# Second mixer: the inverse key norms spread as high and low fp32r parts, in pairs between value columns

## The chip, the cores and the metric

The kernel runs on one core of one Trainium2 chip. The metric is the device time of one execution in microseconds (us); lower is better. Five engines work side by side and meet at semaphores: TensorE (PE; its weight loads are listed apart as PEld), VectorE (DVE), ScalarE (ACT), GpSimd (POOL) and SyncE (SP), which issues the DMAs here.

## The reference, cut to what matters

The kernel computes a two-layer encoder trunk on 256 tokens of width 1024. Layer 0 mixes with a long convolution and windowed attention, layer 1 with a bidirectional RWKV-7 scan; each mixer stands between two half-step feed-forward blocks. The change lies in the mixer of layer 1, in how the keys `kk` are normalised by head (16 heads of 64 channels):

```
kk = (k * k_k).reshape(B, L, H, N)
kk = kk / maximum(norm(kk, axis=-1, keepdims=True), 1e-12)
...
k_dir = k * (1 + (a - 1) * k_a)      # a: two directions
b_dir = kk * a
```

`-kk` and `b_dir` enter the scan that follows, `v` too.

## The kernel before

**Precision.** Most products are computed from fp32 numbers that are split into two fp32r parts: a high part (a rounding copy) and a low part (the number less its high part). `three` (L246 to L248) issues the three matmuls high·high, high·low and low·high. Weights come through `raw` by DMA, one step of three blocks of 1024 columns at a time; ScalarE or VectorE writes the high part `WH` (L189, L195; L2159, L2160), VectorE or GpSimd the low part `WL` (L201, L2168, L210). A matmul of plain fp32 operands appears in the trace as two passes.

**The second mixer's projections** (`pe_mix1`, `act_mix1`, `dve_mix1`) run in the order of blocks written out by hand in `MIX1_ORDER` (L38): keys k0 to k7, receptances r0 to r7, the first halves l0 to l3 of the low-rank nets, values v0 to v7 and the second halves x0, x1 (`pe_lora_out`), with v3 and v4 woven into these. A step is three blocks, so x0 lies in step 7, x1 in step 8, and v5, v6, v7 are the last, ninth step. Each value block k adds, for all eight column groups m of 128, three matmuls into the banks `VB`; `pe_row_block` calls a hook `wait(m // 2)` before every second group.

**The norms.** TensorE sums the squares of a head after r6 (L1450); VectorE limits them (L2253), ScalarE takes the root (L2107), VectorE the reciprocal into `RN[:, 1, :]` (L2237): 16 rows, one for each head, of 256 tokens. `pe_spread_norms` (L1411 to L1416) spreads them: for each of eight tiles j of 128 channels, a 16×128 selector `selt` of ones and zeros times the 16×256 reciprocals gives a 128×256 tile in the banks `XB`. It does all eight in a row, in plain fp32, before the last two column groups of v5 (hook n == 3). `removal_keys` on VectorE (L2267) scales the keys with them, two tiles a call, after waiting until `kk_bc` counts those tiles.

**What stands around it.** ScalarE goes through steps n = 2 to 9: at n = 8 the two low-rank hiddens (`hidden`, L2066 to L2070), the split of a weight step (L189, L195), two high parts of inputs (L2050), the sigmoid of the gate's hidden rows (L2110), then 16 sigmoids of x0 (`decays`, L2080); behind the loop 16 more of x1, the high part of the weights of step S_O, and the operands of the scan's tile 0. TensorE's x0 waits before its fifth product until all four hidden pieces are there (`hid_ready`, 4), and before every later group of four for the sigmoids of the group that used its bank.

VectorE's queue behind the loop is: the prefix sums of tile 0, the gate's low parts (L2481, L2485, after ScalarE's high part of step S_O), `removal_keys` for tiles 0 to 3, then the operands of scan tile 0: b (L1838), k (L1841), alpha (L1861), query (L1869), `removal_keys` for tiles 6, 7, 4, 5 (L2267) and the bonus product (L1845). GpSimd scales b and k behind VectorE (L2007, L2012, L2014) and then makes a low part of weights (L210). TensorE's first scan tile (L1481) needs alpha, query, scaled b and ScalarE's first copy of V out of the banks (L2128, after v7). VectorE masks its two products (L1916), and the scan goes on from there, tile after tile, with VectorE and TensorE in turn.

The memory of `HX[:, 4:8]` lies unused by the inputs in this mixer; the squares of the keys and then the operands of tile 0 (among them the prefix sums, alpha, query and b) have their places in it.

Of the kernel before, what the change touches and what calls it, by code (L numbers as in the profile page):

```python
# [15 lines left out]
P = 128  # L16
C = 1024
L = 256
CT = C // P
# [78 lines left out]
def build(nc, io):  # L98
    fp32 = mybir.dt.float32
    f32r = mybir.dt.float32r  # L100
    ALU = mybir.AluOpType
# [4 lines left out]
    with ctx:  # L106
        def sb(name, shape, dt=fp32):
            return ctx.enter_context(nc.sbuf_tensor(name, shape, dt))

        def sem(name):  # L110
            return ctx.enter_context(nc.semaphore(name))
# [3 lines left out]
        HX = sb("HX", [P, CT, 2, L], f32r)  # L115
# [32 lines left out]
        def ccols(name, n, off=0):  # L148
            return cst[:, CC[name] + off:CC[name] + off + n]
# [491 lines left out]
        RN = sg[0:16, :, :]  # L641
# [5 lines left out]
        selt = ccols("selt", CT * P)[0:16, :].rearrange("p (j c) -> p j c", c=P)  # L647
# [650 lines left out]
        def by_unit(a):  # L1298
# [4 lines left out]
        xt_ready, xt_hh, xt_hl = sem("xt_ready"), sem("xt_hh"), sem("xt_hl")  # L1303
        k_read, rp_read, va_read = sem("k_read"), sem("rp_read"), sem("va_read")
        omk_ready = sem("omk_ready")
        hid_ready = sem("hid_ready")
        lr_done = sem("lr_done")
        lr_ready = sem("lr_ready")
        lr_hi, lr_lo = sem("lr_hi"), sem("lr_lo")
        kk_sq, kk_ss, kk_max, kk_root, kk_rec, kk_bc, kk_ready = (sem(f"kk_{n}") for n in  # L1310
                                                                "sq ss max root rec bc ready".split())
# [20 lines left out]

        LEAD = 4
        WINDOW = {2: (6, 7, 8), 3: (9, 10), 4: (11, 12), 5: (13, 14), 6: (15, 16), 7: (17, 18), 8: (19, 20), 9: (21, 22, 23)}
        KB, RB4, VB = bank[4:8], bank[0:4], [bank[6], bank[7], bank[0], bank[1]]
        LB, XB = bank[4:6], bank[2:6]

        def pair_half(bs, j):
            return bs[j // 2][:, (j % 2) * L:(j % 2) * L + L]
# [9 lines left out]
        def pe_row_block(pe, slot, b, outs, i, k, wait=None):  # L1349

            for _ in pe_row_steps(pe, slot, b, outs, i, k, wait):
                pass
# [43 lines left out]
        def pe_square_sums(pe):  # L1396

            for k in range(CT):
                if k % 2 == 0:
                    pe.wait_ge(pair_sq, k // 2 + 1)  # L1400
                last = nc.tensor.matmul(stats_bank(4)[:, 0:L], ones, XSQ[:, k, :], start=k == 0, stop=k == CT - 1)
            last.then_inc(st_ready, 1)
# [5 lines left out]
            wait_block(pe, s, b)  # L1408
            yield from pe_row_steps(pe, s % 2, b, VB, 2 * CT + k, k)

        def pe_spread_norms(pe):  # L1411

            pe.wait_ge(kk_rec, 1)
            pe.wait_ge(lr_ready, 32)
            for j in range(CT):
                nc.tensor.matmul(pair_half(XB, j), selt[:, j, :], RN[:, 1, :], start=True, stop=True).then_inc(kk_bc, 1)  # L1416

        def pe_mix1(pe):
            pe_square_sums(pe)
            for g, (name, k) in enumerate(MIX1_ORDER):  # L1420
                s, b, k = S_RKV + g // 3, g % 3, int(k)
                slot = s % 2
                if name == "v" and k in (3, 4):
                    continue
                wait_block(pe, s, b)
                if name == "k":
                    pe_row_block(pe, slot, b, KB, k, k)
                elif name == "r":
                    pe_row_block(pe, slot, b, RB4, CT + k, k)
                elif name == "v":  # L1430
                    wait = None
                    if k == 0:

                        pe.wait_ge(kk_max, 1)
                        wait = lambda n: pe.wait_ge(rp_read, n - 1) if n >= 2 else None
                    if k == 5:
                        wait = lambda n: pe_spread_norms(pe) if n == 3 else None
                    pe_row_block(pe, slot, b, VB, 2 * CT + k, k, wait)
                elif name == "l":
                    if k == 0:  # L1440
                        pe.wait_ge(k_read, 2)
                    pe_lora_in(pe, slot, b, k)
                else:
                    pe_lora_out(pe, slot, b, k, pe_value_steps(pe, 3 + k))
                if (name, k) == ("r", 6):

                    pe.wait_ge(k_read, 4)
                    pe.wait_ge(kk_sq, CT)
                    for j in range(CT):
                        last = nc.tensor.matmul(KB[2][0:16, 0:L], sel[:, j, :], KSQ[:, j, :], start=j == 0, stop=j == CT - 1)  # L1450
                    last.then_inc(kk_ss, 1)
            pe.wait_ge(kk_ready, 2)
            pe.wait_ge(va_read, 1)
            tiles(lambda t, p, c, a: pe_tile(pe, t, p, c, a))


            for i in range(NCH):
                pe_r_whole(pe, CT - 1, 1, i)
                pe_o(pe, i // 2, (4 * (i % 2), 4 * (i % 2) + 1))
                pe_u(pe, CT - 1, i)  # L1460
                pe_o(pe, i // 2, (4 * (i % 2) + 2, 4 * (i % 2) + 3))
                pe_s(pe, CT - 1, 1, i)
                pe_y(pe, CT - 1, 1, i)
                if i < 3:
                    pe_spread(pe, i + 2)
            pe_groupnorm(pe)
# [364 lines left out]
        def dve_kb_wait(dve, t):  # L1831

            dve.wait_ge(ka_ready, t + 1)
            if not (isinstance(t, int) and t < 2):
                dve.wait_ge(tr_done, 3 * t - 3)

        def dve_b(t, p, z):
            return nc.vector.tensor_tensor(BB[p][:, z * L:(z + 1) * L], tile_of(AG, t, z), tile_of(KK, t), ALU.mult)  # L1838
# [198 lines left out]
        def act_mix1(act):  # L2037
            A, cp = nc.scalar.activation, ACT.Copy
# [46 lines left out]
            for n in range(2, RKV_STEPS):  # L2085
                if n == 4:
                    act.wait_ge(blocks_done, past(SLOT[CT - 1]))
                    for j in range(4):
                        A(K[:, 2 * j * L:(2 * j + 2) * L], KB[j][:, :], cp).then_inc(k_read, 1)
                if n == 8:  # L2090
                    hidden()
                if n < 9:
                    next_hi(act, S_RKV + n)
                if n == 7:
                    act.wait_ge(blocks_done, past(SLOT[2 * CT - 1]))
                    for j in range(4):
                        A(R[:, 2 * j * L:(2 * j + 2) * L], RB4[j][:, :], cp).then_inc(rp_read, 1)
                for i in WINDOW[n]:
                    hi(i)
                if 3 <= n < 7:  # L2100
                    for j in (2 * n - 6, 2 * n - 5):
                        hi_triple(j)
                if n in (4, 5):
                    squares(range(4 * n - 16, 4 * n - 12))
                if n == 6:
                    act.wait_ge(kk_max, 1)
                    A(RN[:, 0, :], KSQ[0:16, 0, :], ACT.Sqrt).then_inc(kk_root, 1)  # L2107
                if n == 8:
                    for m in range(2):
                        A(GS[:, m, :], pair_half(LB, 2 + m), ACT.Sigmoid).then_inc(hid_ready, 1)  # L2110
                    decays(0)
                    act.wait_ge(hid_ready, 4)
                    A(GH[:, :, :], GS[:, :, :], cp).then_inc(lr_hi, 1)
# [28 lines left out]
        def dve_mix1(dve, own):  # L2142
            V_ = nc.vector
            tt, ts, stt = V_.tensor_tensor, V_.tensor_scalar, V_.scalar_tensor_tensor
# [87 lines left out]
            for n in range(2, RKV_STEPS):  # L2232
                for i in WINDOW[n]:
                    mix(i)
                if n == 7:
                    dve.wait_ge(kk_root, 1)
                    V_.reciprocal(RN[:, 1, :], RN[:, 0, :]).then_inc(kk_rec, 1)  # L2237
                if n == 8:
                    for i in range(2):
                        dve.wait_ge(lr_hi, i + 1)  # L2240
                        tt(PL[:, i, :], HID[:, i, :], PH[:, i, :].bitcast(fp32), ALU.subtract).then_inc(lr_lo, 1)
                low(n)
                for i in WINDOW[n]:
                    lo(i)
                if 3 <= n < 7:
                    for j in (2 * n - 6, 2 * n - 5):
                        lo_triple(j)
                if n < 6:
                    for j in (2 * n - 4, 2 * n - 3):
                        mix_triple(j)  # L2250
                if n == 6:
                    dve.wait_ge(kk_ss, 1)
                    ts(KSQ[0:16, 0, :], KB[2][0:16, 0:L], 1e-24, None, ALU.max).then_inc(kk_max, 1)  # L2253
# [20 lines left out]
            dve.wait_ge(lr_ready, 32)  # L2274
            dve.wait_ge(rp_read, 4)
            dve_kb_wait(dve, 0)
            own(dve_b(0, 0, 0))
            dve_b(0, 0, 1).then_inc(bb_ready, 1)
            own(dve_k(0, 0, 0))
# [502 lines left out]
```

## Time and profile before

| | |
|---|---|
| median of 3 runs | 1232.78 us (1232.63 to 1235.1) |
| the profiled execution: its time | 1232.91 us |
| its span, first to last instruction | 1231.1 us |
| busy: TensorE, VectorE, ScalarE, GpSimd | 97%, 65%, 53%, 33% of the span |
| mean granted TensorE clock | 0.993 |

Times in the rows are us from the span's start. A matmul's duration in a row is longer than the distance to the next start, because matmuls overlap; the distance between starts is what a stream costs. In a row of the timeline, "x8" is eight instructions in a row merged into one, and a bracket at the end tells how long the engine stood idle before them and what ended that. The granted clock of 1.00 is 2.4 GHz and 0.50 is 1.2 GHz.

### The profile page before, as it was taken

The numbers are of one execution on the slowest core, as the hardware profiler recorded it, in microseconds if no ns is written. First come the engines' busy times: TensorE is split into PE (matmuls) and PEld (weight loads), VectorE is DVE, ScalarE is ACT, GpSimd is POOL, SyncE is SP. The second block draws the span as 40 slices with busy tenths as digits, with TensorE's granted clock in tenths as the row PEclk, the third lists the DMA queues.
The fourth block names the chain that finished last, engine by engine and source line by source line (L and its number), as shares of the span: only waits on it lengthen the run. The fifth ranks groups of instructions, "written<-read, shape, count | busy, mean of one in ns | idle before, by whom it ended". The sixth has DMA issues, their size and how long they took to land.

```text
span 1231.1 us, 27446 instructions
## 1 busy us (share of the span) xinstructions
PE 1195.8 (97%) x11182; PEld 1084.4 (88%) x11182; DVE 797.2 (65%) x1265; ACT 655.2 (53%) x1114; POOL 403.2 (33%) x218
## 2 busy tenths in 40 slices
PE   8999999988999999999999989998999999999998
PEld 6899999876989999999999979987999889999998
DVE  7655555788585555485555569878777758755554
ACT  5545444654275454474545446684666654554452
POOL 0343443311123434424343410005343412334433
PEclk9999999999999999999999989999999999999999
DMA  9345455422255454555545434411000025554452
GB/s 364 142 167 204 166 191 205 154 103 104 103 205 180 178 204 163 195 208 203 187 170 204 165 142 156 184 73 54 4 4 3 3 75 189 206 201 174 184 200 90
DMA packets 18657, 188.04 MB, mean 153 GB/s; under 512 B 2064, under 2 KB 2576, under 8 KB 3600
## 3 DMA queue, kind: packets, MB, share of 16 engines
q1 hardware_dynamic: 18576, 186.87, 41.2%
q8 instruction: 61, 1.00, 0.3%
q14 instruction: 20, 0.16, 0.0%
HBM read 185.82 MB, written 1.05 MB: 152 GB/s over the span
## 4 chain that ended last, share of the span: by engine, by line
PE 84%; DVE 9%; ACT 5%; issue 1%; DMA 0%; SPq 0%; DVEq 0%; ACTq 0%
PE gu_bank L267 24%; PE gu_bank L269 12%; PE bank L246 7%; PE bank L248 7%; PE bank L247 7%; PE bank L1481 7%; PE gu_bank L246 4%; PE gu_bank L247 3%; PE gu_bank L248 3%; PE gu_bank L1481 3%; DVE WL L201 2%; PE gu_bank L1512 2%; ACT WH L189 2%; DVE HX L407 1%; PE bank L940 1%
## 5 line engine op out<-in xcount | busy, mean ns | idle before, releaser
L210 POOL TENSOR_TENSOR WL<-raw,WH 128x1024 fp32r<-128x1024 f32 x96 | 325.7, 3393 | 587.0 <-ACT WH L195 565.4
L267 PE MATMUL gu_bank<-HX,WH 128*128 128x512 f32 x1280 | 455.6, 398 | 1.2 <-DVE PL L548 1.2
L269 PE MATMUL gu_bank<-HX,WL 128*128 128x256 f32 x1280 | 359.5, 281 | 0.0
L201 DVE TENSOR_TENSOR WL<-raw,WH 128x2048 fp32r<-128x2048 f32 (+1 forms) x113 | 242.9, 2149 | 123.3 <-ACT WH L189 123.3
L267 PEld LDWEIGHTS gu_bank<-HX,WH 128*128 128x128 f32 x1280 | 240.7, 188 | 57.5 <-DVE PL L548 1.8
L269 PEld LDWEIGHTS gu_bank<-HX,WL 128*128 128x128 f32 x1280 | 241.9, 189 | 0.0
L189 ACT ACTIVATE WH<-raw 128x2048 fp32r<-128x2048 f32 (+1 forms) x113 | 203.0, 1797 | 23.4 <-PE gu_bank L248 14.4
L246 PE MATMUL bank<-PH,WH 128*128 128x256 f32 (+1 forms) x720 | 202.3, 285 | 0.0
L247 PE MATMUL bank<-PL,WH 128*128 128x256 f32 (+1 forms) x720 | 201.6, 283 | 0.0
L248 PE MATMUL bank<-PH,WL 128*128 128x256 f32 (+1 forms) x720 | 201.5, 283 | 0.0
L246 PE MATMUL gu_bank<-HX,WH 128*128 128x256 f32 x464 | 137.4, 296 | 3.2 <-DVE HX L407 3.0
L246 PEld LDWEIGHTS bank<-PH,WH 128*128 128x128 f32 (+1 forms) x720 | 135.2, 190 | 4.9 <-ACT work L2110 0.2
L467 ACT ACTIVATE work<-gu_bank 128x512 f32<-128x512 f32 x80 | 48.0, 600 | 170.1 <-PE gu_bank L269 170.1
L248 PEld LDWEIGHTS bank<-PH,WL 128*128 128x128 f32 (+1 forms) x720 | 135.4, 190 | 0.0
L247 PEld LDWEIGHTS bank<-PL,WH 128*128 128x128 f32 (+1 forms) x720 | 135.4, 190 | 0.0
L533 DVE TENSOR_TENSOR gu_bank<-gu_bank,work 128x512 f32<-128x512 f32 x80 | 56.0, 700 | 119.7 <-ACT work L467 119.1
L247 PE MATMUL gu_bank<-HX,WH 128*128 128x256 f32 x464 | 132.0, 284 | 0.0
L248 PE MATMUL gu_bank<-HX,WL 128*128 128x256 f32 x464 | 131.7, 284 | 0.0
L195 ACT ACTIVATE WH<-raw 128x1024 fp32r<-128x1024 f32 x113 | 118.3, 1047 | 0.0
L472 ACT ACTIVATE work<-gu_bank 128x256 f32<-128x256 f32 x84 | 32.3, 385 | 128.6 <-DVE gu_bank L543 128.6
L246 PEld LDWEIGHTS gu_bank<-HX,WH 128*128 128x128 f32 x464 | 89.6, 193 | 9.8 <-issue 5.6
L247 PEld LDWEIGHTS gu_bank<-HX,WH 128*128 128x128 f32 x464 | 89.8, 193 | 0.4 <-issue 0.2
(314 smaller groups left out, 1808.9 us busy)
## 6 DMA issues: line engine op xcount, KB each, us to landing
raw<-stream_in SPq DMA_DIRECT2D x114, 1536.0 KB, 6.4
cst<-const_in SPq DMA_DIRECT2D x1, 1600.0 KB, 17.3
X<-xT_in SPq DMA_DIRECT2D x1, 1024.0 KB, 5.9
raw<-stream_in SPq DMA_DIRECT2D x1, 1024.0 KB, 7.9
arena<-hconst_in SPq DMA_DIRECT2D x2, 512.0 KB, 11.2
out<-X SPq DMA_DIRECT2D x4, 256.0 KB, 2.1
arena<-hconst_in SPq DMA_DIRECT2D x1, 768.0 KB, 14.2
arena<-fw_in SPq DMA_DIRECT2D x1, 512.0 KB, 8.7
```

The costliest lines, as they stand in the source:

```text
L189: nc.scalar.activation(WH[:, slot, :cut], raw[:, slot, :cut], ACT.Copy).then_inc(hi_ready, 1)
L195: nc.scalar.activation(WH[:, slot, cut:end], raw[:, slot, cut:end], ACT.Copy).then_inc(hi_last, 1)
L201: nc.vector.tensor_tensor(WL[:, slot, :cut], raw[:, slot, :cut], WH[:, slot, :cut].bitcast(fp32), ALU.subtract).then_inc(lo_ready, 1)
L210: (eng or nc.gpsimd).tensor_tensor(WL[:, slot, cut:end], raw[:, slot, cut:end], WH[:, slot, cut:end].bitcast(fp32), ALU.subtract).then_inc ...
L246: nc.tensor.matmul(out_ap, wh, xh, start=start, stop=False, **kw)
L247: nc.tensor.matmul(out_ap, wh, xl, start=False, stop=False, **kw)
L248: return nc.tensor.matmul(out_ap, wl, xh, start=False, stop=stop, **kw)
L267: nc.tensor.matmul(out[:, :], WH[:, slot, w:w + P], HX[:, x, :, :].rearrange("p i t -> p (i t)"), start=k == 0, stop=False)
L269: return nc.tensor.matmul(out[:, L:2 * L], WL[:, slot, w:w + P], HH[:, x, :], start=False, stop=k == CT - 1)
L467: nc.scalar.activation(gus[o], gu_bank[:, o, :, L:2 * L], ACT.Copy).then_inc(gx_ready, 1)
L533: nc.vector.tensor_tensor(gated, gu_bank[:, o, :, 0:L], gus[o], ALU.add).then_inc(gsum_ready, 1)
L1481: last = nc.tensor.matmul(dst[r, cols], w[r], x[r], start=start, stop=stop)
```

## The change

The reciprocals are split into a high part `RNH` (a rounding copy on ScalarE) and a low part `RNL` (a subtraction on VectorE); the selector is copied to fp32r as `SELR` on ScalarE. All three lie in the first 16 partitions of `HX[:, 4:8]`. A spread is then two fp32r matmuls into one sum, and the eight spreads are issued in pairs: before the last two column groups of v5, and before the first, third and fifth column group of v6. Since `SELR` and the parts lie where VectorE later writes b, alpha and query, VectorE waits for all eight spreads (`kk_bc`, 8) before it writes b.

```
+        spent = HX[0:16, 4:8, :, :].rearrange("p k i t -> p (k i) t")
+        RNH, RNL, SELR = spent[:, 2, :], spent[:, 3, :], spent[:, 4:8, :].rearrange("p j (i c) -> p (j i) c", c=P)
...
-        def pe_spread_norms(pe):
-            pe.wait_ge(kk_rec, 1)
-            pe.wait_ge(lr_ready, 32)
-            for j in range(CT):
-                nc.tensor.matmul(pair_half(XB, j), selt[:, j, :], RN[:, 1, :], start=True, stop=True).then_inc(kk_bc, 1)
+        def pe_spread_norms(pe, js):
+            if js[0] == 0:
+                pe.wait_ge(kk_parts, 3)
+                pe.wait_ge(lr_ready, 32)
+            for j in js:
+                nc.tensor.matmul(pair_half(XB, j), SELR[:, j, :], RNH, start=True, stop=False, skip_group_check=True)
+                nc.tensor.matmul(pair_half(XB, j), SELR[:, j, :], RNL, start=False, stop=True, skip_group_check=True).then_inc(kk_bc, 1)
...
                     if k == 5:
-                        wait = lambda n: pe_spread_norms(pe) if n == 3 else None
+                        wait = lambda n: pe_spread_norms(pe, (0, 1)) if n == 3 else None
+                    if k == 6:
+                        wait = lambda n: pe_spread_norms(pe, (2 * n + 2, 2 * n + 3)) if n < 3 else None
...
                 if n == 8:
+                    act.wait_ge(kk_rec, 1)
+                    A(RNH, RN[:, 1, :], cp).then_inc(kk_parts, 1)
+                    A(SELR, selt, cp).then_inc(kk_parts, 1)
                     for m in range(2):
                         A(GS[:, m, :], pair_half(LB, 2 + m), ACT.Sigmoid).then_inc(hid_ready, 1)
                     decays(0)
...
+                if n == 9:
+                    dve.wait_ge(kk_parts, 2)
+                    tt(RNL, RN[:, 1, :], RNH.bitcast(fp32), ALU.subtract).then_inc(kk_parts, 1)
...
             dve_kb_wait(dve, 0)
+            dve.wait_ge(kk_bc, CT)
             own(dve_b(0, 0, 0))
```

## Rows read from the trace of the kernel before

**Rows 1.** Chain of waits, 780 to 880 us: start, us, engine, output, line

```profile
824.41 1.92 PE gu_bank L1416 x8
...
838.55 1.98 PE gu_bank L1481 x32
```

**Rows 2.** Windows: stretch, us, busy us and count by engine, granted clock, DMA

```profile
824.28:828.70 4.42, 4.42 (x18) 3.50 (x16) 3.73 (x7) 4.39 (x7) 0.00 (x0) 0.77 0.00 0
828.70:833.70 5.00, 5.00 (x23) 4.51 (x22) 4.97 (x11) 1.31 (x4) 3.74 (x3) 0.52 0.00 0
833.70:837.82 4.12, 4.12 (x35) 3.92 (x33) 3.49 (x5) 0.00 (x0) 3.25 (x2) 1.00 0.00 0
...
246.00:248.00 2.00, 2.00 (x10) 1.67 (x10) 2.00 (x2) 0.00 (x0) 0.00 (x0) 1.00 0.00 0
...
298.00:299.00 1.00, 0.00 (x0) 0.00 (x0) 0.53 (x3) 0.64 (x4) 0.00 (x0) 1.00 0.00 0
```

**Rows 3.** Timeline of TensorE around the spreads: start, duration, line, output<-inputs, shape, count

```profile
824.13 0.28 PE L248 MATMUL gu_bank<-HX,WL 128*128 128x256 f32 x1
...
829.19 0.58 PE L246 MATMUL gu_bank<-HX,WH 128*128 128x256 f32 x1
...
837.54 0.28 PE L248 MATMUL gu_bank<-HX,WL 128*128 128x256 f32 x1
```

**Rows 4.** Timeline of TensorE in x0, where 64-row and 128-row weights take turns

```profile
805.93 0.39 PE L246 MATMUL bank<-PH,WH 64*128 64x256 f32 x2
...
806.28 0.28 PE L248 MATMUL bank<-PH,WL 64*128 64x256 f32 x2
806.49 0.39 PE L246 MATMUL bank<-HX,WH 128*128 128x256 f32 x1
806.71 0.28 PE L247 MATMUL bank<-HX,WH 128*128 128x256 f32 x1
806.83 0.28 PE L248 MATMUL bank<-HX,WL 128*128 128x256 f32 x1
```

**Rows 5.** Timeline of ScalarE in step 8, and its first copy of V

```profile
802.24 1.06 ACT L195 ACTIVATE WH<-raw 128x1024 fp32r<-128x1024 f32 x1
803.19 0.72 ACT L2050 ACTIVATE HX<-work 128x256 fp32r<-128x256 f32 x2
803.93 1.28 ACT L2110 ACT_TABLE_LOAD   x1
805.22 0.66 ACT L2110 ACTIVATE work<-bank 128x256 f32<-128x256 f32 x2
...
837.86 0.60 ACT L2128 ACTIVATE arena<-gu_bank 128x512 f32<-128x512 f32 x1 [6.53 <-PE gu_bank L248]
```

**Rows 6.** Timeline of VectorE from step 9 to the first masks of scan tile 0

```profile
812.60 1.23 DVE L2159 CAST WH<-raw 128x2048 fp32r<-128x2048 f32 x1 [4.92 <-PE bank L248]
...
824.84 1.23 DVE L2481 TENSOR_TENSOR WL<-raw,WH 128x1024 fp32r<-128x1024 f32 x1 [2.64 <-ACT WH L189]
...
827.47 1.66 DVE L2267 SCALAR_TENSOR_TENSOR arena<-arena,par,gu_bank 128x256 f32<-128x256 f32 x4
829.04 0.76 DVE L1838 TENSOR_TENSOR scan<-arena 128x256 f32<-128x256 f32 x2
...
831.17 2.26 DVE L1869 TENSOR_TENSOR scan<-arena,XSQ 128x256 f32<-128x256 f32 x2
...
835.03 2.19 DVE L1845 SCALAR_TENSOR_TENSOR XSQ<-arena,par,XSQ 128x256 f32<-128x256 f32 x1
839.68 0.42 DVE L1916 TENSOR_TENSOR scan<-gu_bank,cst 128x256 f32<-128x256 f32 x1 [2.45 <-PE gu_bank L1481]
840.55 0.42 DVE L1916 TENSOR_TENSOR scan<-gu_bank,cst 128x256 f32<-128x256 f32 x1 [0.45 <-PE gu_bank L1481]
```

**Rows 7.** Timeline of GpSimd: its split behind the operands of tile 0

```profile
834.54 2.40 POOL L210 TENSOR_TENSOR WL<-raw,WH 128x1024 fp32r<-128x1024 f32 x1
```

**Rows 8.** All instructions of line L1845: duration in ns, least, median, most

```profile
L1845 DVE SCALAR_TENSOR_TENSOR XSQ<-arena,par,XSQ x8: 475/480/2195, 835.0 to 976.4; 128x256 f32<-128x256 f32 x8
```

More of the change, by code:

```diff
@@ L1305, in build @@
         omk_ready = sem("omk_ready")
+        kk_parts = sem("kk_parts")
         hid_ready = sem("hid_ready")
```

## The prediction

> **What bounds the kernel now.** I began with the chain of waits over the second mixer's projections. Up to 838 us it is nearly all TensorE, and the eight spreads of the inverse norms stand in it [rows 1]: eight fp32 passes of 256 columns take 1.92 us, 0.24 each, where an fp32r matmul of that width starts every 0.12 us [rows 4]. The windows view shows a second cost: the granted clock falls from 1.00 to a mean of 0.77 in the stretch of the spreads and 0.52 in the next 5.00 us, while TensorE is never idle, and is back at 1.00 after 833.70 [rows 2]; 0.50 is the lower of the two levels, 1.2 GHz. In TensorE's timeline the last column before the spreads starts at 824.13 and the first behind them at 829.19, 4.94 us later than the pitch of 0.12 would put it; the other 53 starts of v5 to v7 take 8.35 us where 53 × 0.12 is 6.36, so the low clock costs 2.0 us more [rows 3].
>
> Then the stretch's other engines. From 838.55 the chain is the first scan tile on TensorE, then VectorE [rows 1]. VectorE's timeline shows its slack: it finishes its operands of tile 0 at 837.22 (835.03 + 2.19), waits 2.45 us for the tile's first product, and 0.45 us for the second [rows 6]. **Those 2.9 us are all that an earlier TensorE can give here**; then VectorE is the bound, unless it gets earlier too.
>
> **The change part by part.** *Sixteen fp32r matmuls for eight fp32 ones*, in four bursts of four. Their own pitch is bounded by 0.12 and 0.24 us; I take 0.12, since the 64-row fp32r pairs stream at it too. But a burst changes the height of the weights from 128 rows to 16 and back. At the nearest such change, 64 to 128 rows, starts stand 0.21 and 0.22 us apart before 0.12 returns [rows 4], 0.19 us lost per change; bounds 0 and 0.19, and I take 0.19, as the fp32 passes came no sooner than 0.21 us after a 128-row matmul either (0.28 in the chain's modelled ends, 824.13 to 824.41) [rows 1, 3]. Counted from 824.13: the last of the sixteen is the 34th start, behind seven changes: 34 × 0.12 + 7 × 0.19 = 5.41, so 829.54, ended at 829.82. The 36 remaining value matmuls and the eighth change bring the last start to 834.05 and V's end to 834.33, against 837.82 (837.54 + 0.28) [rows 3]: 3.49 us earlier, with the clock at 1.00 throughout.
>
> *Two copies on ScalarE*, ahead of the gate's sigmoid in step 8. By the split of 1024 columns (802.24 to the next start at 803.19) the selector's copy is 0.95 us; by two copies of 256 in 0.72, the norms' is 0.36 [rows 5]. Sixteen partitions save nothing I can see; together 1.3 us, bounds 0.7 and 1.5. Nothing hides it: ScalarE runs copies, a table load to 805.21 and the sigmoids to 805.88 without a gap [rows 5], and TensorE's fifth low-rank product starts at 805.93, because it waits for all hidden rows [rows 4]. So TensorE's low-rank blocks, both rounds of sigmoids queued on ScalarE, the split of the next weights behind them and VectorE's work behind that all come 1.3 us later: VectorE waits 2.64 us for that split before 824.84 [rows 6]. The wait for the reciprocal ahead of the copies costs nothing; VectorE made it a step earlier.
>
> *One subtraction on VectorE* (16×256) in step 9: the 4.92 us that VectorE idles before its cast at 812.60 hide it [rows 6]; without that cover about 0.4 us.
>
> *TensorE's wait for the parts* replaces that for the reciprocal and is long met. *The pair-wise order* lets the first keys' scaling begin as before, at 827.47: VectorE is busy with the gate's low parts until then [rows 6], so it never waited for the spreads.
>
> *VectorE's new wait for all eight spreads* stands before the b operands, which start at 829.04 [rows 6]. With the last spread ended at 829.82 they wait 0.78 us (0 without change losses). Queued behind are the k, alpha and query operands, the remaining keys and the bonus product; GpSimd's operands wait for the b operands, and TensorE's tile for alpha and query (833.43 = 831.17 + 2.26, + 1.3 + 0.78 = 835.51).
>
> **Sum.** VectorE is ready for tile 0 at 837.22 + 1.3 + 0.78 = 839.30. TensorE: V ends at 834.33 + 1.3 = 835.63; from V's end to the tile now takes 0.73 us (837.82 to 838.55, through ScalarE's first copy of V [rows 1, 5]), so 836.36, its first product 1.13 us later (838.55 to 839.68) at 837.49, the second 0.87 after it. VectorE therefore comes last. Its first mask moves from 839.68 to 839.30, 0.38 us, and the second's wait of 0.45 goes: **0.83 us gained**. From there the chain is VectorE's and only shifts. The profiled execution took 1232.91 us (span 1231.1 and 1.8 around it), 0.13 above the median of 1232.78; 1232.08 by its own clock, 1232.0 as a median. What can be told from no change here is about 0.2%, 2.5 us.
>
> **What decides beyond that.** The clock's fall came with TensorE busy for all 4.42 us of the stretch [rows 2]. The Trainium skill, "TensorE: Matmul & The Clock Gate", section "HAM oscillation — how this bites in real kernels", ties such falls to gaps in which TensorE idles; the trace disagrees with it here. By that rule the spreads are not the cause, and the low clock would stay: the second rival's time.
>
> VectorE's bonus product takes 2.195 us here against a median of 0.480 [rows 8], and ends just after GpSimd's split (834.54 + 2.40 = 836.94) [rows 6, 7]. It is held by GpSimd; both follow from the b operands and move together, so I keep it. The Trainium skill, "SBUF — State Buffer", section "Who interferes with whom", states a lock that goes to whoever issues first; the trace agrees.
>
> **Rivals.** *The hold dissolves*: if VectorE reaches the bonus product before 834.54's split, that is 0.5 us earlier relative to GpSimd, 1.72 us go: 2.55 gained, 1230.2. Against it: nothing in the change moves them apart. *TensorE decides*: V's lead lands whole, 2.2 us with the copies on the path, 3.5 with them hidden: 1229.3 to 1230.6. For it: the spreads stand in the chain; against it: VectorE's 837.22, which the change only delays.
>
> *The last pair comes late, slower than before.* Place: VectorE's new wait. If 16-row fp32r passes cost 0.24, the change does not do what it says, and four bursts come 4 × 4 × 0.12 = 1.92 us later: 1.09 lost, 1233.9. If instead the clock falls among them as now (0.77 over 4.42 us is 2.0 us at 0.50, so from about 826.7), what is left to 829.54 doubles: 2.9 later, 2.0 lost, 1234.8. It decides once the last spread is more than 0.83 us later than summed. For it: the fall under 16-row passes; against: ten such passes around 246 us left the clock at 1.00 [rows 2], and the bursts are 0.5 us each.
>
> *The stall lowers the clock*: TensorE now idles 1.3 us at the sigmoids; 6.8 us at half speed (2.0 + 0.48 × 2 × 5.00) cost 3.4, and all engines follow: 2.6 lost, 1235.4. Against it: a whole idle us at 298 left 1.00 [rows 2].
>
> **Chances.** The sum 0.62 (own range 1230.6 with both losses at their low ends, 1232.4 with the copies at 1.5 and a median as noisy as now); TensorE decides 0.10; the hold dissolves 0.08; late last pair 0.15; stall 0.05. A range of 1229.9 to 1235.0 leaves out half of TensorE's case and the stall, with margins some 0.13. Faster by over 0.2% means below 1230.3: half of each fast rival and a margin, 0.13. Slower, above 1235.25: the stall and a tail of the late pair, 0.08. The rest, 0.79, is no change.
>
> **Right or wrong.** Right if the granted clock stays at 1.00 from 824 to 838; V ends some 2.2 us earlier; ScalarE's sigmoid starts 1.3 us later and TensorE idles there; VectorE idles under 1 us before the b operands; and its waits of 2.45 and 0.45 us are gone. Wrong if VectorE still waits for the tile's first product (then TensorE decides), if the bonus product takes 0.48 us, or if the sixteen start 0.24 us apart.

## The result, and the profile after

The changed kernel is slower: 1239.18 us in the median of 12 runs (1234.46 to 1242.70) against 1233.61 us for the kernel before beside it, a ratio of 1.0033 with a 95% interval of 1.0020 to 1.0045; it is taken over the runs and not from the two medians, whose quotient is 1.0045. Run once more in a second comparison it took 1237.76 us against 1233.56, 1.0024 (1.0007 to 1.0041). The forecast of 1232.0 us had the wrong sign, and its range ended at 1235.0. The profiled execution shown here took 1240.07 us with a span of 1238.3.

I read the result from TensorE outwards. First its own timeline, at the fifth low-rank product of x0, around the first burst of spreads and to the end of V (columns as in [rows 3]; the bracket is the idle time ahead and what ended it):

```profile
809.72 0.39 PE L246 MATMUL bank<-PH,WH 64*128 64x256 f32 x2 [1.28 <-ACT work L2120]
...
831.34 0.28 PE L248 MATMUL gu_bank<-HX,WL 128*128 128x256 f32 x1
831.55 0.38 PE L1420 MATMUL gu_bank<-HX 16*128 16x256 f32 x1
831.77 0.28 PE L1421 MATMUL gu_bank<-HX 16*128 16x256 f32 x1
831.89 0.27 PE L1420 MATMUL gu_bank<-HX 16*128 16x256 f32 x1
832.01 0.27 PE L1421 MATMUL gu_bank<-HX 16*128 16x256 f32 x1
832.21 0.39 PE L246 MATMUL gu_bank<-HX,WH 128*128 128x256 f32 x1
832.44 0.28 PE L247 MATMUL gu_bank<-HX,WH 128*128 128x256 f32 x1
...
841.24 0.28 PE L248 MATMUL gu_bank<-HX,WL 128*128 128x256 f32 x1
845.04 3.01 PE L1488 MATMUL gu_bank<-scan 64*64 64x128 f32 x32 [3.52 <-DVE scan L1876]
```

The spreads do what they were summed to do: starts 0.12 us apart inside a burst, and 0.21 and 0.22 us at the change of weight height. From the last start ahead of them to V's last start it is 9.90 us (831.34 to 841.24), where it was 13.41 [rows 3]. Then comes what was not foreseen: TensorE, done with V, stands idle for 3.52 us and waits for VectorE's query operand (L1876).

The granted clock of the same stretches, in the windows view (columns as in [rows 2]):

```profile
812.00:821.00 9.00, 9.00 (x45) 7.09 (x44) 1.43 (x2) 4.16 (x13) 0.00 (x0) 0.50 0.21 86
...
822.00:845.00 23.00, 19.52 (x154) 16.77 (x152) 19.05 (x29) 16.04 (x33) 6.08 (x4) 1.00 0.00 1
845.00:848.00 3.00, 2.96 (x35) 2.99 (x37) 2.17 (x6) 0.45 (x2) 0.18 (x1) 0.63 0.82 258
```

The fall among the spreads [rows 2] is gone: 1.00 from 822 to 845. But two others are there, nine microseconds at 1.2 GHz in x0 and x1, and one in the scan's first tile.

ScalarE's timeline shows what stands ahead of the first:

```profile
806.35 0.40 ACT L2117 ACTIVATE HX<-work 16x256 fp32r<-16x256 f32 x1
806.65 1.04 ACT L2118 ACTIVATE HX<-cst 16x1024 fp32r<-16x1024 f32 x1
807.72 1.28 ACT L2120 ACT_TABLE_LOAD   x1
809.01 0.66 ACT L2120 ACTIVATE work<-bank 128x256 f32<-128x256 f32 x2
```

The two copies (L2117, L2118) take the 1.37 us from 806.35 to 807.72 in front of the table load, and TensorE's fifth low-rank product at 809.72 waits 1.28 us for the sigmoid behind them.

VectorE's timeline from the first scaled keys to the masks of tile 0, against [rows 6]:

```profile
834.67 1.66 DVE L2280 SCALAR_TENSOR_TENSOR arena<-arena,par,gu_bank 128x256 f32<-128x256 f32 x4
837.14 0.76 DVE L1845 TENSOR_TENSOR scan<-arena 128x256 f32<-128x256 f32 x2 [0.81 <-PE bank L1421]
837.82 1.84 DVE L1848 TENSOR_TENSOR XSQ<-XSQ,arena 128x256 f32<-128x256 f32 x2
839.59 1.29 DVE L1868 SCALAR_TENSOR_TENSOR scan<-arena,scan 128x256 f32<-128x256 f32 x2
840.80 3.98 DVE L1876 TENSOR_TENSOR scan<-arena,XSQ 128x256 f32<-128x256 f32 x2
844.70 1.65 DVE L2280 SCALAR_TENSOR_TENSOR arena<-arena,par,bank 128x256 f32<-128x256 f32 x4
846.38 0.48 DVE L1852 SCALAR_TENSOR_TENSOR XSQ<-arena,par,XSQ 128x256 f32<-128x256 f32 x1
846.78 0.42 DVE L1923 TENSOR_TENSOR scan<-gu_bank,cst 128x256 f32<-128x256 f32 x1
848.08 0.42 DVE L1923 TENSOR_TENSOR scan<-gu_bank,cst 128x256 f32<-128x256 f32 x1 [0.88 <-PE gu_bank L1488]
```

The new wait costs 0.81 us, as summed (0.78). Behind it four groups change their length: the k operands (L1848) take 1.84 us, alpha (L1868) 1.29, the query 3.98 where it was 2.26 [rows 6], and the bonus product (L1852) 0.48 where it was 2.19 [rows 6]. From the start of b to the end of the query it is 7.64 us (837.14 to 844.78); before it was 4.39 (829.04 to 833.43). So the operand that TensorE's tile needs last comes **3.25 us later after b.** On VectorE itself 1.71 us of that come back, because the bonus product is no longer held, and the first mask (846.78) follows it without a wait; the second waits 0.88 us for TensorE.

GpSimd's timeline shows what VectorE waited for:

```profile
837.98 1.40 POOL L2014 TENSOR_TENSOR scan<-scan,XSQ 128x512 f32<-128x512 f32 x1 [114.78 <-DVE scan L1845]
839.74 0.86 POOL L2019 TENSOR_TENSOR XSQ<-XSQ 128x256 f32<-128x256 f32 x1 [0.36 <-DVE XSQ L1848]
840.67 1.34 POOL L2021 TENSOR_TENSOR XSQ<-XSQ 128x512 f32<-128x512 f32 x1
841.98 2.52 POOL L210 TENSOR_TENSOR WL<-raw,WH 128x1024 fp32r<-128x1024 f32 x1
```

Lay the two side by side. GpSimd's scaling of b ends at 839.38, VectorE's k at 839.66; its next operation ends at 840.60, alpha at 840.88; its split ends at 844.50, the query at 844.78. Three times the operation of VectorE that was under way ends 0.28 us behind GpSimd's. The kernel before, run again as a control at the end of the study, shows the other order; VectorE, then GpSimd:

```profile
829.92 0.75 DVE L1838 TENSOR_TENSOR scan<-arena 128x256 f32<-128x256 f32 x2
830.59 0.75 DVE L1841 TENSOR_TENSOR XSQ<-XSQ,arena 128x256 f32<-128x256 f32 x2
831.26 0.75 DVE L1861 SCALAR_TENSOR_TENSOR scan<-arena,scan 128x256 f32<-128x256 f32 x2
832.04 2.26 DVE L1869 TENSOR_TENSOR scan<-arena,XSQ 128x256 f32<-128x256 f32 x2
...
835.90 2.19 DVE L1845 SCALAR_TENSOR_TENSOR XSQ<-arena,par,XSQ 128x256 f32<-128x256 f32 x1
```

```profile
830.75 2.40 POOL L2007 TENSOR_TENSOR scan<-scan,XSQ 128x512 f32<-128x512 f32 x1 [107.72 <-DVE scan L1838]
833.11 0.91 POOL L2012 TENSOR_TENSOR XSQ<-XSQ 128x256 f32<-128x256 f32 x1
834.10 1.35 POOL L2014 TENSOR_TENSOR XSQ<-XSQ 128x512 f32<-128x512 f32 x1
835.41 2.40 POOL L210 TENSOR_TENSOR WL<-raw,WH 128x1024 fp32r<-128x1024 f32 x1
```

There it is GpSimd that is held: its scaling of b takes 2.40 us instead of 1.40, while k and alpha pass at 0.75. The query ends 0.28 us behind GpSimd's second operation (834.02, 834.30), the bonus product 0.28 behind the split (837.81, 838.09). With the change GpSimd stands further ahead: its b holds the second k, its second operation alpha, its third and the long split the query.

### The profile page after: what moved, and what is told of

Its sections match the earlier page's. It is cut to its first block, busy times and chain, and to the rows that moved or that the text cites. A ratio compares the mean times of both kernels' runs of the same rounds, so it can differ in the third digit from the quotient of the medians.

```text
span 1238.3 us, 27449 instructions
## 1 busy us (share of the span) xinstructions
PE 1198.9 (97%) x11182; PEld 1087.9 (88%) x11182; DVE 798.8 (65%) x1266; ACT 655.1 (53%) x1116; POOL 401.6 (32%) x218
## 4 chain that ended last, share of the span: by engine, by line
PE 82%; DVE 10%; ACT 6%; issue 1%; DMA 0%; SPq 0%; DVEq 0%; ACTq 0%
PE gu_bank L267 23%; PE gu_bank L269 12%; PE bank L246 7%; PE bank L1488 7%; PE bank L248 7%; PE bank L247 7%; PE gu_bank L246 3%; PE gu_bank L1488 3%; PE gu_bank L247 3%; PE gu_bank L248 3%; DVE WL L201 2%; ACT WH L189 2%; PE gu_bank L1519 2%; DVE HX L407 1%; ACT WH L195 1%
```

## The experiments

**How they are compared.** Single runs scatter by several microseconds and the medians by up to 2 (before, in five comparisons: 1233.56 to 1235.60), so I also measured a stage in each profile: from the first tanh of the low-rank hiddens (the last mark ahead of everything that the change touches in step 8) to the first mask of scan tile 1. Before, that is 57.91 us, in the control 57.88. What follows the stage is 373.75 to 374.10 us in every kernel but one (e4: 374.74), so nothing there depends on the change. What lies ahead of the stage moves more: of the 7.2 us between the spans of the first two profiles 4.76 lie in the stage and 2.54 ahead of it, in work that the change does not touch. There the granted clock of the change has a mean of 0.79 from 24 to 32 us and from 752 to 760, where before has 1.00; the two other falls ahead of the stage (728 to 740, and one between 268 and 296) are in both. "Low clock" gives where 4-us windows of the stage were below 1.00.

| kernel | idle before b | query | stage | low clock, us | ratio (95%) |
|---|---|---|---|---|---|
| before | 0 | 2.26 | 57.91 | 824–836 | |
| after | 0.81 | 3.98 | 62.67 | 808–824, 844–852 | 1.0033 (1.0020–1.0045) |
| e1 copies early | 0.80 | 3.98 | 58.84 | 836–848 | 1.0012 (0.9997–1.0026) |
| e2 stall only | 0 | 2.28 | 57.50 | 828–836 | 1.0010 (0.9993–1.0026) |
| e3 row, copies early | 0 | 2.27 | 54.68 | none | 0.9993 (0.9979–1.0008) |
| e4 short stall | 0.8 | 3.98 | 59.99 | 852–864 | 1.0018 (1.0006–1.0030) |
| e5 wait earlier | 0 | 2.26 | 57.03 | 844–852 | 1.0004 (0.9992–1.0016) |
| e6 row and a wait | 2.81 | 3.96 | 60.61 | 828–848 | 1.0034 (1.0022–1.0046) |
| e7 split first | 0 | 2.27 | 55.11 | none | 0.9997 (0.9985–1.0008) |
| e8 row, copies late | 0 | 2.29 | 55.96 | none | 0.9994 (0.9983–1.0006) |
| e10 split later | 0 | 2.29 | 57.62 | 824–832, 848–852 | 1.0008 (0.9994–1.0023) |
| e11 = e3 again | 0 | 2.29 | 55.50 | 848–856 | 0.9996 (0.9984–1.0008) |
| e12 = after again | 0.80 | 3.98 | 59.70 | 840–848 | 1.0024 (1.0007–1.0041) |
| e13 = before again | 0 | 2.26 | 57.88 | 824–836 | 0.9994 (0.9982–1.0006) |

**e1: the change with the two copies moved out of step 8.**

```
-                if n == 8:
+                if n == 7:
                     act.wait_ge(kk_rec, 1)
                     A(RNH, RN[:, 1, :], cp).then_inc(kk_parts, 1)
                     A(SELR, selt, cp).then_inc(kk_parts, 1)
+                if n == 8:
                     for m in range(2):
```

> The changed kernel with ScalarE's two copies one step earlier, in the 1.75 us that it idles before the first tanh. Theory (the copies in step 8 stall TensorE 1.28 us and the clock falls behind the stall): TensorE idles under 0.2 us at the sigmoids, the clock stays at 1.00 through x0 and x1, and the kernel is 2 us faster than before (ratio 0.998). Rival (the pairs, or VectorE's wait for all eight spreads, cost it): the clock may be up, but the kernel stays 1 to 4 us slower than before (1.001 to 1.003).

The copies go into time that ScalarE idled (its wait ahead of the first tanh is 0.52 us instead of 1.75). The stall at the sigmoids goes, TensorE's V ends 3.5 us earlier than before from the first tanh on (its first copy at 35.06 us, against 38.58), and still the kernel is no faster than before: 1236.88 us. The query takes 3.98 us with a clock of 1.00 up to 836. The copies are therefore not the whole cause; my first theory, that they were, fell here.

**e2: the kernel before with the two copies in step 8 and nobody who reads them.**

```
...
                 if n == 8:
+                    act.wait_ge(kk_rec, 1)
+                    A(RNH, RN[:, 1, :], cp).then_inc(kk_parts, 1)
+                    A(SELR, selt, cp).then_inc(kk_parts, 1)
```

> The kernel before with the two copies alone added in step 8; nothing reads them, the spreads stay fp32 and in a row. Theory: TensorE stalls 1.3 us; in the runs whose clock then falls to 0.50 in x0 the kernel is 4 to 5 us slower (1.0035), in the others 1.3 us (1.001). Rival (pairs): within 0.1% of before, as nothing of the spreads is changed.

The same 1.28 us of idle TensorE, the sigmoid 7.18 us behind the tanh as in the change (7.19; before 5.94), and the clock stays at 1.00 behind it. The b operands start 1.23 us later, at 30.99 us; the query takes 2.28. VectorE's wait for the tile's first product takes the delay up: it is 0.85 us, where before has 2.45 [rows 6]. The stage is even 0.4 us shorter than before's, but the low clock behind the fp32 spreads was shorter too (4-us windows of 0.89 and 0.68, against 0.84, 0.50 and 0.81). So the stall alone made no loss here; what it costs at an equal clock this profile does not show, and the ratio fits both expectations.

**e3: e1 with all sixteen spreads in a row, ahead of v5's last two columns.**

```
                     if k == 5:
-                        wait = lambda n: pe_spread_norms(pe, (0, 1)) if n == 3 else None
-                    if k == 6:
-                        wait = lambda n: pe_spread_norms(pe, (2 * n + 2, 2 * n + 3)) if n < 3 else None
+                        wait = lambda n: pe_spread_norms(pe, range(CT)) if n == 3 else None
```

> As the first, with all sixteen fp32r spreads in one row where the fp32 ones stood. Theory: the row keeps the clock, needs two changes of weight height instead of eight, and VectorE waits no more before b: 3 us faster than before (0.9975), about 0.8 us faster than with pairs. Rival (pairs are what keeps the clock): the granted clock falls behind the sixteen as it does behind the fp32 spreads, and the kernel is no faster than with pairs.

The spreads end before VectorE needs them, it does not pause, the query is 2.27 us again, and the stage is 3.2 us shorter than before's. In the median that is 1233.06, and in e11, the same kernel once more, 1233.18:

> e3_row_early once more, for a narrower interval. Its stage of the second mixer was 3.2 us shorter than before's at the same clock; if nothing later gives that back, the ratio is 0.9974 to 0.9985 over runs whose low clocks fall alike. If the clock's other stretches swallow it, 0.999 to 1.000.

Both intervals take in 1. The stage's gain of 2.4 to 3.2 us is 0.2%, at the edge of what a comparison can tell. The first tanh came at 802.47 and 801.74 us in these two, at 799.28 and 800.17 in the two profiles of before, and at 800.01 and 800.13 in e7 and e10, which have the early copies too. The windows show what goes with it: the clock fell between 24 and 32 us in all profiles but these four, and in none of the four (24 to 32 us: 1.00). Kernels that are the same as before up to step 8 have that fall as well (after, e2, e8, e12), so it does not come from the early copies; what decides on it the runs leave open.

**e4: the change with only the selector's copy moved out of step 8.**

```
-                if n == 8:
+                if n == 7:
                     act.wait_ge(kk_rec, 1)
-                    A(RNH, RN[:, 1, :], cp).then_inc(kk_parts, 1)
                     A(SELR, selt, cp).then_inc(kk_parts, 1)
+                if n == 8:
+                    A(RNH, RN[:, 1, :], cp).then_inc(kk_parts, 1)
                     for m in range(2):
```

> The changed kernel with only the selector's copy (0.95 us) moved a step earlier, the norms' copy (0.3 us) left in step 8. If the length of TensorE's stall decides whether the clock falls: a stall of 0.3 us, clock 1.00 in x0 in all runs, 1.5 to 2 us faster than before (0.9985). If any stall there lowers it: two groups of runs, 3 us slower in one of them.

The stall shrinks to 0.3 us (the sigmoid at 6.24), the query stays at 3.98, the time at 1237.25. The clock stayed at 1.00 in x0, but fell in tile 0 (852 to 864), and the kernel is slower than before where 1.5 to 2 us faster was expected. A shorter stall does not make up the loss; the query's hold remains.

**e5: e1 with the same wait put two groups of instructions earlier,** before the first scaled keys, so that VectorE idles there and not in front of b.

```
+            dve.wait_ge(kk_bc, CT)
             removal_keys(XB[0], (0, 1))
...
-            dve.wait_ge(kk_bc, CT)
             own(dve_b(0, 0, 0))
```

> The first experiment (copies a step earlier, pairs kept) with VectorE's wait for all eight spreads moved ahead of the first keys' scaling, so that b follows the scaling without a pause. There b started 30.65 us behind the first tanh and the query ended at 38.29. Theory (a pause of VectorE right before b lets GpSimd take the memory port first, and its split then holds the query): b starts about 32.2, 1.5 us later, and yet the query ends at 36.6, 1.7 us earlier; k takes 0.76 us, the query 2.3. Rival (a later b is simply later): the query ends at 39.9 and the kernel is 1.5 us slower than the first experiment.

This is the run that decides. VectorE's timeline:

```profile
833.21 1.66 DVE L2281 SCALAR_TENSOR_TENSOR arena<-arena,par,gu_bank 128x256 f32<-128x256 f32 x4 [2.40 <-PE bank L1421]
834.78 0.76 DVE L1845 TENSOR_TENSOR scan<-arena 128x256 f32<-128x256 f32 x2
835.46 0.76 DVE L1848 TENSOR_TENSOR XSQ<-XSQ,arena 128x256 f32<-128x256 f32 x2
836.13 0.76 DVE L1868 SCALAR_TENSOR_TENSOR scan<-arena,scan 128x256 f32<-128x256 f32 x2
836.91 2.26 DVE L1876 TENSOR_TENSOR scan<-arena,XSQ 128x256 f32<-128x256 f32 x2
```

VectorE now waits three times as long (2.40 us), and starts b 1.46 us later than e1 counted from the tanh, yet its query ends 1.79 us earlier (36.50 against 38.29): from b to the query's end it is 4.39 us as before, against 7.64. What costs is not the wait's length but that it stands directly in front of b.

**e6: the counterpart.** e3 has no pause before b; here it gets one, by a wait for v6 that the result does not need.

```
             dve.wait_ge(kk_bc, CT)
+            dve.wait_ge(blocks_done, past(MIX1_ORDER.index("v6")))
             own(dve_b(0, 0, 0))
```

> The third experiment (copies a step earlier, spreads in a row) with one wait added on VectorE, before b, for v6 on TensorE: a pause of about 1.25 us and nothing else. Theory: the order on the port turns round as with the pairs, k takes 1.85 us and the query 3.98; the query ends 38.6 us behind the first tanh instead of 34.14, and the kernel is 3 to 4 us slower than the third (ratio to before 1.002). Rival (the bursts of the pairs, not the pause, cost it): the query ends at 35.4 and the kernel is at most 1.25 us slower than the third.

VectorE's timeline, then GpSimd's:

```profile
834.65 0.76 DVE L1843 TENSOR_TENSOR scan<-arena 128x256 f32<-128x256 f32 x2 [2.81 <-PE gu_bank L248]
835.33 1.85 DVE L1846 TENSOR_TENSOR XSQ<-XSQ,arena 128x256 f32<-128x256 f32 x2
...
838.30 3.96 DVE L1874 TENSOR_TENSOR scan<-arena,XSQ 128x256 f32<-128x256 f32 x2
```

```profile
835.48 1.41 POOL L2012 TENSOR_TENSOR scan<-scan,XSQ 128x512 f32<-128x512 f32 x1 [110.64 <-DVE scan L1843]
...
839.46 2.52 POOL L210 TENSOR_TENSOR WL<-raw,WH 128x1024 fp32r<-128x1024 f32 x1
```

The row of spreads is untouched, and the pause alone brings back the whole pattern: k 1.85, the query 3.96, GpSimd's scaling at 1.41, and a time of 1238.20 us. The pause is longer than the 1.25 us that I expected (2.81), so the query ends at 40.26 and not at 38.6; of the 6.1 us that it comes later than in e3, 2.9 are b's later start and 3.2 the changed order (7.61 us from b to the query's end, against 4.39). In e3, e7, e8, e10 and e11 the wait for the spreads stands in front of b as well, but is met before VectorE comes, and the order is the old one: it is the pause that turns it round, not the wait as such. e5 and e6 together show the cause.

**e7: e1 with GpSimd's split ahead of its operands of tile 0.**

```
             split_last(pool, S_RKV)
+            split_last(pool, S_O, order=True)
             for part in range(2):
                 pool_operands(pool, 0, 0, part)
-            split_last(pool, S_O, order=True)
```

> The first experiment with GpSimd's split of weights (2.4 us) moved ahead of its operands of tile 0, so that it can't hold the query. Theory: the query takes 1 to 1.5 us instead of 3.98 and ends 35.8 to 36.6 us behind the first tanh instead of 38.29; TensorE idles under 2 us there, its clock stays at 1.00 in tile 0, 2 us faster than the first experiment (ratio to before 0.9995). Rival (the query waits for something else): it ends at 38.3 as before.

The split now meets VectorE's low part for the gate and stretches that instead:

```profile
826.82 3.28 DVE L2500 TENSOR_TENSOR WH<-raw,WH 32x1024 fp32r<-32x1024 f32 x1
```

3.28 us for 1.22 in the other kernels. The delay swallows the pause before b: the spreads are done when VectorE comes. The query takes 2.27 and the bonus product 0.48, and the time is 1232.95. The query ends at 36.22, as expected, but not for the expected reason alone: with the pause gone GpSimd's scaling of b is held again (2.41 us) and holds the query in its turn. So this run does not separate the split from the pause. The hold of the split is moved to a place where there was a wait to pay for part of it.

**e8: the change with the spreads in a row, its copies still in step 8** (the edit of e3, on the changed kernel).

> The changed kernel, copies in step 8, with the spreads in one row: the fourth corner of copies early or late by row or pairs. From the first tanh to the first mask of tile 1 the kernel before took 57.91 us, the changed one 62.67, copies early with pairs 58.84, copies early in a row 54.68. Theory (two separate losses): 1.25 us of stall on top of the last, 55.9, and up to 3.4 more where the clock falls behind the stall: 55.9 to 59.3, at or below before. Rival (the late copies alone explain the loss): 61 or more.

Stage 55.96 us, 1233.38 in the median: with the stall of 1.28 us in place, only the bursts are undone (and with them the pause), and the loss is gone. The stall stood in this profile with the clock at 1.00 throughout.

**e10: e3 with GpSimd's split behind its work of tile 0.**

```
             nc.gpsimd.tensor_tensor(BSUM[:, :, :], ...).then_inc(bs_ready, 1)
+            if isinstance(t, int) and t == 0:
+                split_last(pool, S_O, order=True)
...
-            split_last(pool, S_O, order=True)
             pool.wait_ge(blocks_done, 3 * S_O)
```

> The spreads in one row and the copies early (as in e3_row_early), and GpSimd's split of 1024 columns taken from behind the operands of tile 0 to behind its last addition in tile 0. Both theories: the bonus product takes 0.48 us instead of 2.12, the first mask of tile 0 comes some 36.1 us behind the first tanh (e3: 37.79). If a hold only costs where VectorE has no slack, and GpSimd's idle 3.8 us in tile 0 is a free place: first mask of tile 1 at 53.0 (e3: 54.68, before 57.91), time 1231.5, ratio about 0.998. If GpSimd's split holds whatever VectorE does at its side: one of VectorE's short operations of tile 0 (0.3 to 0.9 us in e3) takes 2 to 2.5 us instead, and the first mask of tile 1 is at 54.7 to 55.3, the time e3's.

The bonus product falls to 0.48 us as expected, but the first mask of tile 0 comes at 37.24 us and not at 36.1, after 1.00 us of waiting for TensorE, whose clock was low behind the spreads. And the split finds another victim, an operand of tile 1; VectorE, then GpSimd:

```profile
844.79 2.50 DVE L1843 TENSOR_TENSOR raw<-arena 128x256 f32<-128x256 f32 x1
```

```profile
844.28 2.72 POOL L210 TENSOR_TENSOR WL<-raw,WH 128x1024 fp32r<-128x1024 f32 x1
```

In e3 that operand took 0.88 us. GpSimd's idle time was no free place: VectorE was at work there. The stage of 57.62 us is above both expectations; two low stretches of the clock (0.63 in the window from 828, 0.57 in that from 848) stand in it too, so how much of it the hold made is not settled.

**e12 and e13: the changed kernel and the kernel before once more.**

> The changed kernel once more, to see what repeats. Order on the port (my theory): the query takes 3.9 to 4.0 us and the second k 1.8 again, the bonus product 0.48, whatever the clock does. The stall: ScalarE's sigmoid 7.2 us behind the first tanh again; whether the clock falls behind it is open: 0.50 over some 10 us as in the first profile, or 1.00 as in e2_stall_only and e8_row_late. Stage to the first mask of tile 1: 62.7 with the fall, 59 to 60 without. Ratio 1.002 to 1.005.

> The kernel before, unchanged, as a control: ratio 1.000 with an interval of about 0.0013 to each side. What is open is how much of a difference between two profiles belongs to the chip. If only the stage of the second mixer differs between the kernels, the first tanh comes at 800.0 to 803.8 us here as in all other profiles (799.28 in the first), and from it to the first mask of tile 1 it is 57.5 to 58.4 us again. If the low clock beside the fp32 spreads moves from run to run, that stage scatters by 2 us or more, and a comparison of single profiles at this place is worth little.

The query's 3.98 us, k's 1.84 and the stall of 1.28 are the same to the hundredth. The clock does not. Windows of e12, where the first profile had 0.50 over nine microseconds:

```profile
810.00:820.00 10.00, 8.72 (x82) 6.82 (x78) 4.16 (x9) 7.94 (x20) 0.00 (x0) 1.00 0.43 159
820.00:830.00 10.00, 9.39 (x80) 7.82 (x78) 7.82 (x14) 8.60 (x21) 0.00 (x0) 1.00 0.01 2
```

So the change costs 1.8 us in its stage without that fall (59.70 less 57.91) and 4.8 with it (62.67); a shorter fall in tile 0 is in both. By the two ratios the kernel is 3.0 and 4.1 us slower, between the two. The control repeats before's stage to 0.03 us, its spreads with 0.50 from 828 to 834 included.

## Why the prediction was wrong

Its terms, in its own order:

- *The spreads' pitch and the change of weight height*: 0.12 and 0.19 us, both measured so. V was to come 3.49 us earlier; 3.51 in TensorE's timeline. Right.
- *The clock at 1.00 in the stretch of the spreads*: right in both profiles of the change. That the fp32 spreads alone had lowered it is less sure: the clock fell behind them in all three profiles that have them, but also behind the fp32r row in two of five (e6 0.67, e10 0.63, 828 to 832), with TensorE busy throughout; in the six with pairs it did not. [Rows 1] has only the first eight of the sixteen fp32 passes; the other eight took 2.93 us, in part at the low clock. The sum goes by starts and is not touched by that.
- *The two copies*: 1.3 us summed, 1.25 on the sigmoid, 1.28 as TensorE's idle time. Right, and so was V's end with both terms: 36.35 us from the first tanh by the sum, ScalarE's first copy of V at 36.30 in e12.
- *The new wait*: 0.78 us summed, 0.81 and 0.80 measured. Right.
- *The step that failed*: "It is held by GpSimd; both follow from the b operands and move together, so I keep it." They do not move together once the wait stands in front of b. I had a pair of rows that showed who holds whom [rows 6, 7], and treated the order as a property of the code. The runs show that it hangs on what VectorE does just before: working straight on into b, it passes with k and alpha while GpSimd waits 1.0 us; idle before b, the second k has to wait already, and from there every operand up to the query. e5 takes the pause away from b and the loss goes; e6 puts one there and it comes.
- *VectorE comes last, and from there the chain only shifts*: half of this held. The first mask has no wait for TensorE in either profile of the change, but it comes 1.6 us later than summed: the sum has the query's end 36.2 us and the first mask 40.0 us behind the tanh, e12 has 39.5 and 41.6 (3.3 us late on the query, 1.7 won back on the bonus product). The second half fell with the step above: TensorE's tile needs the query, so V's lead is spent as 3.5 us of idle time, and the second mask waits 1.28 us for TensorE in e12 (0.88 in the first profile), where no wait was summed. In place of 0.83 us gained the stage is 1.8 us longer; a low clock in tile 0 (0.60 from 844 to 848) stands in that too.
- *The stall lowers the clock*, given 0.05: it happened in one of the two profiles of the change, where the first mask then came 3.3 us later than in the other, near the 3.4 that it was priced at (3.0 us over the stage). In e2 and e8 the same stall left 1.00, so it is one profile of four, and the chance looks too small. The row against it, an idle stretch at 298 [rows 2], was one case taken for a rule: behind the same stretch, 2.65 us long, the clock fell in e6, e7, e10 and e12. The timeline and the windows of e7:

```profile
298.85 1.11 PE L910 MATMUL bank<-cst,arena 128*128 128x128 f32 x4 [2.65 <-DVE arena L1160]
```

```profile
298.50:302.00 3.50, 3.15 (x7) 1.89 (x8) 2.83 (x4) 0.63 (x2) 0.00 (x0) 0.54 0.00 0
```

- *The rivals of the late last pair* named the right place, VectorE's new wait, and the wrong price: the last pair was on time. (What the prediction calls the second rival's time in its sentence on the clock is the 1234.8 of this one.)

The prediction had named the sign: "Wrong … if the bonus product takes 0.48 us". It expected that to be a gain. The bonus product did become shorter; the split it had waited for held the query instead, and the query is on TensorE's path.

The Trainium skill, "SBUF — State Buffer", section "Who interferes with whom", says that issue order decides which of VectorE and GpSimd blocks on the ports that they share. The rows agree that one of the two is held, and ends 0.28 us behind the other. On the order they agree in the change, where the second k (from 838.2) starts behind GpSimd's scaling (837.98) and is held. In the control they do not: there the scaling starts at 830.75 and alpha at 831.26, and yet alpha passes in its 0.75 us and the scaling takes 2.40. The measurement decides: which of the two starts first in the rows does not settle which is held. The kernel before shows the same pair, so its trace alone could have warned that one pair of rows does not fix the order:

```profile
830.38 0.76 DVE L1861 SCALAR_TENSOR_TENSOR scan<-arena,scan 128x256 f32<-128x256 f32 x2
```

```profile
829.88 2.40 POOL L2007 TENSOR_TENSOR scan<-scan,XSQ 128x512 f32<-128x512 f32 x1 [107.76 <-DVE scan L1838]
```

In the control and in the change alike GpSimd starts its first operation 0.08 us behind b's end (830.67 to 830.75, 837.90 to 837.98); what differs is the pause ahead of b.

## What to carry to other kernels

Where two engines hold each other up, as VectorE and GpSimd do here, a wait can cost more than its length: here it changed who goes first, and the whole sequence behind it. Put it where the instructions directly behind it are not held (here ahead of the scaled keys, which keep their 1.64 us beside a working GpSimd in the control), or let its condition be met early (spreads in a row). And before an engine's stall is priced by its length, lay the two engines' ends side by side: a constant small distance, here 0.28 us, shows who held whom, and what else can be held.

## What was not expected of the hardware

- A pause of 0.8 to 2.8 us ahead of b turned round which engine was held: VectorE's k 0.76 to 1.84 us, its query 2.26 to 3.98 (3.96 in e6), GpSimd's scaling 2.40 to 1.40, in all four kernels with a pause there (after, e1, e4, e6) and in the repeat, and in none of the nine other profiles. How the chip comes to that order the runs do not show.
- The granted clock fell with TensorE busy all the time (control, 828 to 834, 0.50), behind a stall of 1.28 us (after) and not behind the same stall (e2, e8, e12). The runs of one kernel lie 3 to 11 us apart (before, in the last comparison, 1232.44 to 1238.72), and a difference of 0.2% needs the stage read from the profile beside the medians.
- No version measured is clearly faster than the kernel before. The nearest, with the spreads in a row, stands at 0.9993 and 0.9996 (0.9994 with the copies late), and all three intervals take in 1.
